# RWKV chain: the first chunk without state products, the state array cleared once by GpSimd

## The reference, cut to what matters

```python
def wkv7_scan(r, w, k, v, a, b):
    B, _, H, N = r.shape
    def step(state, inp):
        r_t, w_t, k_t, v_t, a_t, b_t = inp
        sa = jnp.einsum('bhvk,bhk->bhv', state, a_t)
        state = (state * w_t[:, :, None, :] + sa[..., None] * b_t[:, :, None, :]
                 + v_t[..., None] * k_t[:, :, None, :])
        return state, jnp.einsum('bhvk,bhk->bhv', state, r_t)
    state0 = jnp.zeros((B, H, N, N), jnp.float32)
    _, y = lax.scan(step, state0, (tm(r), tm(w), tm(k), tm(v), tm(a), tm(b)))
```

## Time and profile before

| what | us |
|---|---|
| median of three runs | 3294.23 |
| lowest and highest | 3291.33, 3294.79 |
| the profiled execution | 3291.42 |
| its span | 3289.6 |
| mean granted clock of TensorE | 0.914 |
| TensorE busy | 2826.8 (86%) |
| VectorE busy | 2313.7 (70%) |
| ScalarE busy | 1257.3 (38%) |
| GpSimd busy | 813.3 (25%) |

### The profile page before, as it was taken

The page is one execution under the profiler, slowest core; times in us unless marked ns, Lnnn a source line. Parts: engine busy times, 40 slices in busy tenths (PEclk is TensorE's granted clock), DMA queues, the critical chain, the costliest instruction groups (busy, mean ns, idle before and its releaser), DMA issues. The chain is left out here.

```text
span 3289.6 us, 57570 instructions
## 1 busy us (share of the span) xinstructions
PE 2826.8 (86%) x22507; PEld 1834.6 (56%) x22507; DVE 2313.7 (70%) x4080; ACT 1257.3 (38%) x2060; POOL 813.3 (25%) x475
## 2 busy tenths in 40 slices
PE   6896989976899999999699999577787768779987
PEld 3453455545577777777446566356565544334466
DVE  4794377889788888888672677578888843567732
ACT  3232124348333333333312576444454423133221
POOL 0650045530445455555202221100000011000000
PEclk9658999987999999999899999689899978889998
DMA  3001245555999999999333320411111015143140
GB/s 126 1 1 58 103 133 170 172 180 233 360 377 361 362 362 364 362 362 350 126 94 106 88 59 20 136 32 32 32 42 32 20 56 195 58 128 102 51 141 33
DMA packets 278230, 495.00 MB, mean 150 GB/s; under 512 B 18784, under 2 KB 177120, under 8 KB 275872
## 3 DMA queue, kind: packets, MB, share of 16 engines
q1 hardware_dynamic: 241184, 358.24, 32.0%
q0 software_dynamic: 36864, 134.23, 10.4%
HBM read 435.21 MB, written 57.21 MB: 150 GB/s over the span
## 5 line engine op out<-in xcount | busy, mean ns | idle before, releaser
L1347 PE MATMUL banks<-gated_hi,v_hi 128*128 128x384 bf16 (+2 forms) x1536 | 335.0, 273 | 0.5 <-DVE gated_lo L1318 0.5
L1347 PE MATMUL banks<-gated_lo,v_hi 128*128 128x384 bf16 (+2 forms) x1536 | 335.0, 273 | 0.0
L1347 PE MATMUL banks<-gated_hi,v_lo 128*128 128x384 bf16 (+2 forms) x1536 | 335.0, 273 | 0.0
L1185 POOL DMA_INDIRECT gathered_u<-in_u_rows,first_tile_rows x128 | 212.5, 1660 | 288.4 <-DVE gathered_dots L1293 156.5
L815 POOL TENSOR_TENSOR early_u_lo<-early_u_raw,early_u_hi 128x1024 bf16<-128x1024 f32 x64 | 156.0, 2439 | 336.2 <-ACT early_u_hi L875 336.2
L1190 POOL DMA_INDIRECT gathered_v<-in_v,first_tile_rows x128 | 175.3, 1369 | 201.7 <-DVE x_tokens L1285 181.8
L1792 POOL TENSOR_TENSOR gates_w_lo<-gates_raw,gates_w_hi 128x1024 bf16<-128x1024 f32 x24 | 53.4, 2227 | 600.1 <-ACT gates_w_hi L2083 600.1
L1347 PEld LDWEIGHTS banks<-gated_hi,v_hi 128*128 128x128 bf16 x1536 | 150.3, 98 | 56.4 <-issue 1.0
L846 PE MATMUL banks<-act_hi,early_u_hi 128*128 128x384 bf16 x512 | 168.0, 328 | 12.2 <-POOL early_u_lo L815 11.7
L1334 PE MATMUL banks<-act_hi,u_hi 128*128 128x384 bf16 x512 | 168.1, 328 | 11.6 <-DVE u_lo L1271 11.6
L1285 DVE SCALAR_TENSOR_TENSOR x_tokens<-gathered_v,gathered_weights,x_tokens 128x1024 f32<-128x1024 f32 x128 | 164.1, 1282 | 6.1 <-DVE gathered_weights L1276 1.6
(11 more groups left out here) (597 smaller groups left out, 7910.9 us busy)
## 6 DMA issues: line engine op xcount, KB each, us to landing
v_raw<-in_v SPq DMA_DIRECT2D x128, 512.0 KB
early_u_raw<-in_u SPq DMA_DIRECT2D x64, 512.0 KB, 3.9
u_raw<-in_u SPq DMA_DIRECT2D x64, 512.0 KB
gate_tables<-gate_piece SPq DMA_DIRECT2D x12, 2048.0 KB, 6.3
gate_group<-gate_tables SPq DMA_DIRECT2D x32, 768.0 KB
ffn_up_raw<-in_ffn_up SPq DMA_DIRECT2D x20, 1024.0 KB, 7.5
early_gelu<-early_gelu_columns SPq DMA_DIRECT2D x64, 192.0 KB, 1.9
gelu_early_rows<-early_gelu SPq DMA_DIRECT2D x32, 384.0 KB
```

The costliest lines, as they stand in the source:

```text
L1185: pool.indirect_dma_start(gu[:, n % GROUP, :], None, u_table, bass.IndirectOffsetOnAxis(ap=rows.index[:, 0, n:n + 1], axis=0)).then_inc(gu ...
L1347: m = pe.matmul(ps[:, bank, to:to + width], v[:, j, cols], w[:, j, tok:tok + width], start=start and n == 0 and to == 0, stop=stop and n = ...
```

## The change

For chunk 0 the two products with the state (L2337 and L2353) are left out, as the state is zero there; the products that follow start their banks instead of adding to them. TensorE no longer waits for `state0`, and this name leaves the table. The update after chunk 0 multiplies by the factor and adds nothing. VectorE no longer clears `st` and `std` for each pair; GpSimd clears both slots of `st` once at the stage's start, behind its two large clearings, and VectorE waits for that before the first pair's chain.

```diff
@@ rwkv_names
-            "vector": ["state0"] + [n for c in chunks for n in [f"rhs{c}"] + ([f"state{c + 1}"] if c < S // P - 1 else [])
+            "vector": [n for c in chunks for n in [f"rhs{c}"] + ([f"state{c + 1}"] if c < S // P - 1 else [])
@@ gpsimd
                 pool.memset(G2[1], 0.0).then_inc(cleared, 1)
+                pool.memset(st[:], 0.0).then_inc(cleared, 1)
                 for p in range(3 * KD):
@@ vector, chain
                     if part == 0:
                         steps.begin("chain", j)
-                        if isinstance(j, int) and j == 0:
-                            dve.memset(st[:, 1, :], 0.0)
-                        dve.memset(std[:], 0.0)
-                        steps.done("chain", dve.memset(st[:, 0, :], 0.0), "state0", hold=True)
+                        if j == 0:
+                            dve.wait_ge(cleared, 4)
...
                             own = slice(h * HD, (h + 1) * HD)
+                            if c == 0:
+                                ins = dve.tensor_scalar(st[own, 1, own], ps[own, 1, own], fac[own, 0:1], None, ALU.mult)
+                                continue
                             ins = dve.scalar_tensor_tensor(st[own, (c + 1) % 2, own], ps[own, 1, own], fac[own, c:c + 1],
                                                            std[own, own], ALU.mult, ALU.add)
@@ tensor, chain
                     if what == 0:
-                        steps.wait("chain", "vector", j, f"state{c}")
-                        pe.matmul(ps[:, 6, 0:P], a[:, cols], st[:, c % 2, :], start=True, stop=False)
+                        if c >= 1:
+                            steps.wait("chain", "vector", j, f"state{c}")
+                            pe.matmul(ps[:, 6, 0:P], a[:, cols], st[:, c % 2, :], start=True, stop=False)
                         for h, rows in heads:
-                            ins = pe.matmul(ps[:, 6, rows], G[:, 0, h * NCH + c, :], tok[:, 2, c, rows], start=False, stop=h == 1)
+                            ins = pe.matmul(ps[:, 6, rows], G[:, 0, h * NCH + c, :], tok[:, 2, c, rows], start=c == 0,
+                                            stop=c == 0 or h == 1)
...
-                        pe.matmul(ps[:, 7, cols], r[:, cols], st[:, c % 2, :], start=True, stop=False)
+                        if c >= 1:
+                            pe.matmul(ps[:, 7, cols], r[:, cols], st[:, c % 2, :], start=True, stop=False)
                         for h, rows in heads:
                             out = ps[:, 7, c * P + h * HD:c * P + (h + 1) * HD]
-                            pe.matmul(out, G[:, 1, h * NCH + c, :], uu[:, rows], start=False, stop=False)
-                            ins = pe.matmul(out, G[:, 2, h * NCH + c, :], tok[:, 2, c, rows], start=False, stop=h == 1)
+                            pe.matmul(out, G[:, 1, h * NCH + c, :], uu[:, rows], start=c == 0, stop=False)
+                            ins = pe.matmul(out, G[:, 2, h * NCH + c, :], tok[:, 2, c, rows], start=False, stop=c == 0 or h == 1)
```

## The result

The changed kernel takes 3267.73 us (median; 3265.58 to 3268.41) against 3294.23 before: 26.5 us less. The ratio is 0.992, with a 95% interval of 0.9903 to 0.9937. Timed again later, beside the kernel before, it took 3270.29 against 3293.28. The forecast was 3276.0 with a range of 3270 to 3285, so the first result lies outside it and the later one at its very edge: the sign and the place were right, the size was not. The profiled executions give 3291.42 and 3267.39 us, 24.0 apart, and this is the number that the traces have to explain. The other 2.5 us of the difference of the medians are spread between executions of one and the same kernel: the runs of the kernel before lie up to 3.5 us apart, those of the changed one up to 2.8.

A forecast was written before the change was run, and what follows sets the result against it. The chained turns were taken as paced by latency, a ring of TensorE product, ScalarE copy and VectorE subtraction. 14.3 + 2.4 + 0 + 0 + 1.5 = 18.2 us, so 3294.23 becomes 3276.0, range 3270 to 3285.

The forecast's parts named there:

- Part 1, the wait: Step 1 of turns 1 to 7: TensorE's wait for the cleared state goes, with L2337 of chunk 0; 14.3 us gained.
- The moved wait: Step 1: if the wait fell on `xlx` for both heads, the gain is 1.65 us a turn, 11.6 us.
- the bound of 15.0 us: Upper bound for the removed wait in step 1: 2.08 us in six turns and 2.5 in the first.
- Part 2, the product of `y`: Step 2, ahead of `xlx`: the state product L2353 of chunk 0 goes; 2.4 us gained, bounds 1.5 and 2.65.
- Parts 3 and 4: VectorE's seventeen clearings go: 0 more; GpSimd's one clearing at about 2090.4 us, 0.22 us in proportion: 0.
- Part 5, the clock: Turns 1, 3, 4 and 7: some clock falls go with the second idle; 1.5 us gained, bounds 6.6 either side.
- the case that all of it comes: All four clock falls go: 23.3 us gained, 3271 us; chance 8%.
- The turn that gives nothing: Turn 8: dense passes behind L2337 and L2339 wait for a DMA until 2699.21, so removing the wait gains nothing.
- the second rival: Chain part 0 stays held until about 2261.7 by its other conditions; only matmuls go, 4.5 us, 3289.7; chance 5%.

## Why the prediction was wrong in size

In the stage of the profiled executions, one for each kernel, against the kernel before (us). "Full clock" is what the time from `lx` to `xlx` in steps 1 and 2 shows in undisturbed turns, times seven, and turn 8's 0.2:

```
                                     stage   saved   full clock   rest: clock
changed kernel                       550.0    24.0      16.8           7.2
changed kernel again                 550.0    24.0      16.8           7.2
wait gone, products kept             553.9    20.1      13.4           6.7
products out, wait kept              563.5    10.5       3.3           7.2
only the y product out               577.2    -3.2       1.8          -5.0
before, idle stretch filled          567.4     6.6       0.4           6.2
```

The last column is a sum over all steps, and falls of the clock in other steps hide in it what step 1 does. So here is step 1 alone, from its first product to that of step 2: what it took over full clock in turns 1 to 7, and the turns in which the granted clock fell while it ran:

```
                                     us over full clock    falls in turns
before                                      7.3            1, 3, 4, 7
products out, wait kept                     7.1            1, 2, 4, 5, 6
only the y product out                      6.4            1, 6, 7
before, idle stretch filled                 2.1            1
changed kernel                              1.6            1
changed kernel again                        2.8            1
wait gone, products kept                    1.6            1
clearings kept on VectorE                   2.8            1
```

Where TensorE idles 1.77 us ahead of chain part 0, the clock falls in step 1 in three to five of the seven turns. Where that idle is gone or filled, it falls there in turn 1 alone, which begins with 2.68 us of idle. The products with the state make no difference to this. The 1.2 us more of the two runs with 2.8 come from a fall ahead of step 1 in turn 4.

- **Part 1, the wait.** Right in mechanism, place and the seven turns, and small by 0.8 us: 7 x 2.15 = 15.1 us at full clock in place of 14.3. The moved wait did not fall on `xlx`, as worked out. ScalarE was not late: I let its queue free itself when L2055 and L2142 end (L2053 and L2140 before), but L2142 starts at 2330.97 with L2055's end at 2331.06, and L2134 0.19 us behind the start of L2142. Successive ScalarE instructions overlap here by some 0.1 us, so the queue held nothing up and the bound of 15.0 us was the value.
- **Part 2, the product of `y`.** 0.22 us in step 2 at full clock, 1.8 in eight turns, against 2.4 taken and 2.65 as the upper bound. The prediction's larger values are those of turns at 1.2 GHz, so part of this term was clock. That parts 1 and 2 together come to 16.8 us where 16.7 was forecast is luck: one was too small by about as much as the other was too large. Alone the product bought nothing, as the run with only this product out shows.
- **Parts 3 and 4.** VectorE's clearings off the path and GpSimd's at nothing: both shown, the first by the run that kept them. GpSimd's took 0.31 us against 0.22 in proportion; the line through two sizes in the trace before (0.20 us for 128x128, 2.66 for 128x3072) would have had it.
- **Part 5, the clock, is the step that failed.** I took 1.5 us of the 6.6 that I had worked out for the four falls of step 1, and gave the case that all of it comes 8%. 5.7 us came in step 1 and 7.2 in the stage. 7.2 - 1.5 = 5.7 us is the whole miss in the profiled executions, 24.0 against 18.2. The run with the idle stretch filled shows that step 1's part hangs on the idle: wait, clearing and products kept, and the falls of step 1 go just the same, all but turn 1's. I had the observation (idle, `lx`, idle, fall) and the price, and then discounted it because other idle stretches stay. They did stay and did cost: filling the one in step 2 was worth another 10 us. But they were no reason to expect the falls of step 1 to come back.
- **The turn that gives nothing** in part 1 gave nothing; that chain part 0 had other conditions (the second rival) is refuted by L2342 starting at once.

Two halves of the change gained 23.6 and 8.7 us, more than the whole, and a third one gained nothing for less work. Only the full-clock column adds up (13.4 + 3.3 = 16.7). The clock's part of the stage was +6 to +7 us in four versions and -5 in one, each read from one or two executions. What sets the falls of step 2 and the later steps for a given rhythm stays open: why the run with both products out had fewer of them than the kernel before, and the one with only the `y` product out more, no run here tells.

## What to carry to other kernels

Price an idle stretch of TensorE twice: the wait itself, and the fall of the clock behind it, read from equal stretches at both levels in the same trace. If the idle is what goes, take the falls behind it as gone: here 5.7 of the 7.3 us that they cost in that step came back. In a stage of short products with such stretches a small edit that removes work may come out 5 to 7 us of clock on either side of its sum, so set the range by that, and look whether passes that exist anyway can be put into the gap. Read the clock's part step by step, as its sum over a stage mixes falls of different causes. And look at what runs beside the operation that an engine waits for: here moving two copies in ScalarE's order was worth half as much as the whole change. Look at what it will run beside in its new place too.

## What the runs showed of the hardware

- TensorE at work on useless passes made the kernel faster twice: 6.1 us with six passes a turn in a 1.77 us idle stretch, about 10 us with eight in a 2.25 us one.
- The granted clock fell in step 1 in 9 of the 18 turns numbered 2 to 7 of the three profiles with 1.77 us of idle TensorE in that step (3 before, 4 with both products out, 2 with one), and in none of the 54 of the nine profiles with that idle gone or filled.
- VectorE's predicated copy of 128x512 with both sources in SBUF takes 0.71 us alone and 1.9 to 2.5 us while GpSimd subtracts from SBUF; a VectorE product of 128x512 with both operands in SBUF took 2.5 us instead of 0.69 beside it. VectorE's subtractions with a PSUM operand took at most 0.69 us beside it. The Trainium skill (GPSIMD Engine Reference, section Architecture) says that the two engines share their ports to SBUF; the run with the subtractions moved agrees, with no copy over 0.75 us.
- The time at 1.2 GHz alone doesn't tell the cost. It was 96 us in the version with the subtractions moved and 89 in the changed kernel, which is 13 us slower.
